# Partner rows of the 64-wide rotations: SBUF to SBUF transfers from ScalarE's queue in place of VectorE's shuffle

## The reference, cut to what matters

```python
def apply_rope(x, cos, sin):
    half = x.shape[-1] // 2
    x1, x2 = x32[..., :half], x32[..., half:]
    return jnp.concatenate([x1 * c - x2 * s, x2 * c + x1 * s], axis=-1)

qa = apply_rope(qa.reshape(b, s, A_HEADS, 64), cos_a, sin_a)   # ka, qb, kb alike
iq = apply_rope(iq.reshape(b, s, IDX_HEADS, 32), cos_i, sin_i) # ik alike
dots  = einsum('bqhd,bsd->bqhs', iq, ik) * 32 ** -0.5
score = einsum('bqhs,bqh->bqs', relu(dots), iw * 8 ** -0.5)
_, idx = lax.top_k(score, 128)            # then attention over the chosen keys
```

## Time and profile before

| | |
|---|---|
| median of 3 runs | 3537.01 us (3535.3 to 3541.0) |
| the profiled execution: its time | 3540.26 us |
| the profiled execution: its span | 3538.5 us |
| granted TensorE clock, mean | 0.985 of full speed |
| busy, share of the span: PE / DVE / ACT / POOL | 96% / 52% / 33% / 5% |
| DMA, mean | 93 GB/s |

### The profile page before, as it was taken

How to read it: one execution, slowest core, us unless ns; L and a number is a source line. 1 busy time by engine, 2 the same in 40 slices (tenths; PEclk the granted TensorE clock), 3 DMA queues, 4 the chain that set the end, 5 groups by cost and what they waited for, 6 DMA issues and landing times.

```text
span 3538.5 us, 47550 instructions
## 1 busy us (share of the span) xinstructions
PE 3399.9 (96%) x19436; PEld 2755.4 (78%) x19436; DVE 1830.4 (52%) x2634; ACT 1160.2 (33%) x1744; POOL 162.8 (5%) x136
## 2 busy tenths in 40 slices
PE   8999999999999999998899999999999999999999
PEld 7887786788888888777588888656888877578887
DVE  6667546622343234988642336895323359952233
ACT  2122434522242223342332224345222333542222
POOL 0000000000000000000000002230000023100000
PEclk8999999999999999999999999999999999999999
DMA  6555230122222222210022222210222221112222
GB/s 247 189 190 202 84 110 36 68 99 95 95 102 95 95 95 95 93 61 4 30 90 95 95 95 96 72 60 36 88 102 97 105 83 68 43 54 95 95 96 83
DMA packets 47846, 330.29 MB, mean 93 GB/s; under 512 B 5312, under 2 KB 5568, under 8 KB 9280
## 3 DMA queue, kind: packets, MB, share of 16 engines
q1 hardware_dynamic: 41216, 290.09, 22.5%
q0 software_dynamic: 6464, 37.80, 2.9%
HBM read 325.77 MB, written 2.10 MB: 93 GB/s over the span
## 4 chain that ended last, share of the span: by engine, by line
PE 84%; DVE 11%; ACT 3%; issue 1%; DMA 0%; SPq 0%; DVEq 0%; ACTq 0%
PE PS L2156 25%; PE PS L2158 25%; PE PS L2157 25%; DVE WL L2664 2%; PE PS L338 2%; DVE A L1168 1%; DVE M L1167 1%; PE PS L2234 1%; PE PS L413 1%; PE PS L395 1%; PE PS L343 1%; PE PS L1513 1%; PE PS L951 1%; PE PS L2402 1%; ACT WH L2454 0%
## 5 line engine op out<-in xcount | busy, mean ns | idle before, releaser
L2664 DVE TENSOR_TENSOR WL<-RAW,WH 128x2048 fp32r<-128x2048 f32 x255 | 593.5, 2328 | 302.9 <-ACT WH L2454 302.7
L2454 ACT ACTIVATE WH<-RAW 128x2048 fp32r<-128x2048 f32 x255 | 486.8, 1909 | 189.8 <-PE PS L2158 176.9
L2156 PE MATMUL PS<-EH,WH 128*128 128x512 f32 (+1 forms) x1408 | 535.9, 381 | 5.2 <-DVE X L2787 3.1
L2157 PE MATMUL PS<-EL,WH 128*128 128x512 f32 (+1 forms) x1408 | 534.8, 380 | 0.0
L2158 PE MATMUL PS<-EH,WL 128*128 128x512 f32 (+1 forms) x1408 | 534.8, 380 | 0.0
L2156 PE MATMUL PS<-HH,WH 128*128 128x512 f32 (+1 forms) x1312 | 503.0, 383 | 10.3 <-DVE A L2773 3.4
L2158 PE MATMUL PS<-HH,WL 128*128 128x512 f32 (+1 forms) x1312 | 496.8, 379 | 0.0
L2157 PE MATMUL PS<-HL,WH 128*128 128x512 f32 (+1 forms) x1312 | 496.4, 378 | 0.0
L2703 DVE TENSOR_TENSOR A<-SG,PS 128x512 f32 (+1 forms) x132 | 90.8, 688 | 760.6 <-ACT SG L2586 760.6
L2586 ACT ACTIVATE SG<-PS 128x512 f32<-128x512 f32 x132 | 79.3, 600 | 1062.1 <-PE PS L2158 1062.1
L2156 PE MATMUL PS<-WH,AH 128*128 128x512 f32 x1056 | 412.6, 391 | 0.3 <-DVE CV L2890 0.3
(11 more groups left out here) (436 smaller groups left out, 4222.0 us busy)
## 6 DMA issues: line engine op xcount, KB each, us to landing
RAW<-in_w SPq DMA_DIRECT2D x264, 1024.0 KB, 4.8
E<-in_ada POOLq DMA_DIRECT2D x28, 1024.0 KB, 5.1
E<-in_ada SPq DMA_DIRECT2D x4, 1024.0 KB, 11.4
G<-in_ada SPq DMA_DIRECT2D x4, 1024.0 KB, 20.8
X<-in_x SPq DMA_DIRECT2D x1, 2048.0 KB, 13.3
X<-in_xn POOLq DMA_DIRECT2D x1, 2048.0 KB, 12.1
out_x<-A SPq DMA_DIRECT2D x4, 512.0 KB, 2.7
R<-in_row_ffn_post POOLq DMA_DIRECT2D x4, 256.0 KB, 4.6
```

Of the source, the lines that this page charges most:

```text
L2156: nc.tensor.matmul(out, wh, xh, start=start, stop=False)
L2157: nc.tensor.matmul(out, wh, xl, start=False, stop=False)
L2454: nc.scalar.activation(PLACE[w][0], RAW[:, w % 2, :], ACT.Copy).then_inc(w_hi, 1)
L2664: nc.vector.tensor_tensor(PLACE[w][1], RAW[:, w % 2, :], PLACE[w][0].bitcast(F32), ALU.subtract).then_inc(w_lo, 1)
```

## The change

For the 64-wide rotations VectorE's shuffle is gone. ScalarE, having copied the two tiles of a unit, fetches the partner rows of each by four transfers of 32 partitions by 512 float32 (64 KB each), from `TURN3` to `SIN3`, on its own DMA queue. Partition p receives row p XOR 32, which a shuffle within 32 rows could not give, so the host permutation `halves_met` goes away and the tables are laid out for halves 32 rows apart. VectorE and GpSimd wait for the transfers (`moved`, two semaphores, one for each `SIN3` buffer) where they waited for the shuffle. Before it issues the transfers of rotation n, ScalarE waits until rotation n - 2 is finished. The 32-wide rotations keep the shuffle. The rest of the diff keeps counts.

```diff
@@ act_token_blocks of the first mixer, scalar block
+            t.add("proj", 21)
             t.add("w", 11)
@@ setup
+        moved = sem("moved0"), sem("moved1")
...
+        def swap_done(eng, layer, n):
+
+            if ROPED[n][2] == 64:
+                alike = [x for x, r in enumerate(ROPED) if r[2] == 64 and x % 2 == n % 2]
+                eng.wait_ge(moved[n % 2], 64 * (layer * len(alike) + alike.index(n) + 1))
+            else:
+                alike = [x for x, r in enumerate(ROPED) if r[2] == 32]
+                eng.wait_ge(swapped, layer * len(alike) + alike.index(n) + 1)
@@ pool_mix3
-            n = pool_t.add("m3")
-            pool.wait_ge(m3_loads, 64 * n)
+            layer = pool_t.add("m3") - 1
+            pool.wait_ge(m3_loads, 64 * (layer + 1))
...
-                pool.wait_ge(swapped, n_all)
+                swap_done(pool, layer, n)
                 pool.tensor_tensor(x, x, ROPE[size][0], ALU.mult).then_inc(cos_done, 1)
@@ act_mix3, behind the two copies of unit u
                     ins.then_inc(proj_evac, 1)
+                for n, r in turns_of(u):
+                    if r[2] == 64:
+                        act.wait_ge(proj_evac, proj0 + PROJ3[u][r[1]] + 1)
+                        act.wait_ge(roped, turns0 + n - 1)
+                        for p in range(0, P, 32):
+                            act.dma_start(SIN3[n % 2][p:p + 32], TURN3[n % 3][p ^ 32:(p ^ 32) + 32]).then_inc(moved[n % 2], 16)
@@ dve_mix3, rope
-                nc.vector.stream_shuffle(SIN3[n % 2], TURN3[n % 3], SWAP).then_inc(swapped, 1)
-                dve.wait_ge(swapped, turns0 + n + 1)
+                if r[2] == 32:
+                    nc.vector.stream_shuffle(SIN3[n % 2], TURN3[n % 3], SWAP).then_inc(swapped, 1)
+                swap_done(dve, layer, n)
                 nc.vector.tensor_tensor(SIN3[n % 2], SIN3[n % 2], ROPE[r[2]][1], ALU.mult).then_inc(sin_done, 1)
@@ more_arrays
-            angle = (np.arange(S, dtype=np.float32)[:, None] * inv[None]).T[row % n // 32 * 16 + row % 16]
-            sign = np.where(row % 32 < 16, -1.0, 1.0).astype(np.float32)[:, None]
+            angle = (np.arange(S, dtype=np.float32)[:, None] * inv[None]).T[row % (n // 2)]
+            sign = np.where(row % n < n // 2, -1.0, 1.0).astype(np.float32)[:, None]
@@ matrices
-                part = halves_met(part) if name in ("qa", "ka", "qb", "kb") else part
```

More of the change, by code:

```diff
@@ L1036, in act_mix3 @@
         def act_mix3(act, t, sub, h):
-            w, split, turns0, dots0 = t("w"), h["split"], t("turns"), t("dots")
+            w, split, turns0, dots0, proj0 = t("w"), h["split"], t("turns"), t("dots"), t("proj")
             def read_dots(u, c):
@@ L1082, in act_mix3 @@
             t.add("dots", len(DOTS))
+            t.add("proj", N_PROJ3)
             g0 = t("pairs")
@@ L1741, in act_mix2 @@
             t.add("w", U2)
+            t.add("proj", CHUNKS2)
             def take(to, src, *key):
@@ L3025, in out_units @@
     return down_units(w.reshape(KD, P, D)[order].reshape(D, D))
-def halves_met(w):
-    k, n = w.shape
-    return w.reshape(k, n // 64, 2, 2, 16).transpose(0, 1, 3, 2, 4).reshape(k, n)
 def padded(w, n):
```

## The result

| | median | runs from to | ratio to before, 95% interval | span profiled | clock |
|---|---|---|---|---|---|
| before, same chip | 3536.52 us | 3535.3 to 3542.92 | | 3538.5 | 0.985 |
| after | 3558.47 us | 3557.19 to 3564.79 | 1.0059 [1.0049, 1.0069] | 3563.1 | 0.98 |

The account below looks back on a forecast made before the run. The chain was 84% TensorE, held 3.1 us per layer by VectorE, which has no idle time in passes 9 to 12. Recovering that in two layers, 6.2 us, took 3537.0 to 3530.8 us; range 3526 to 3546 us.

Parts of the forecast that it names:

- In units 2 to 5 this is covered: Units 2 to 5: eight issues, 2.7 us, fit ScalarE's gap before the index dots, leaving 0.5 us.
- The signs: What would show the prediction wrong: ScalarE issues clearly over 0.4 us, landings over 5 us, or longer TensorE waits in attention.
- Everywhere earlier in the layer it waits for others: Before passes 9 to 12 VectorE waits for other engines, so shuffles saved there buy nothing.
- The clock: TensorE falls to 1.2 GHz after idle stretches; nothing in the sum, about 1 us per layer either way.
- my second rival: ScalarE's queue and landings bound passes 10 to 12, and issues overrun before index dots: 6.8 us per layer, 3550.6 us, chance 0.18.
- the loop of passes 10 to 12: Adding, issue, landing, sine, adding: at the upper bounds VectorE, and TensorE too, 4.4 us later per layer.
- The removal: Sixteen shuffles per layer go; the eight in passes 9 to 12 save VectorE 6.2 us, shorter sine products 1.2 us.
- the 0.3 us: Passes 9 to 12: saving per pair of sine products once GpSimd's cosine product is over earlier, 1.2 us per layer.
- The late waits: Passes 9 to 12: VectorE waits for second-rotation transfers, 2.3 us in pass 11, about 1 us in pass 12.
- my 3.2 us: Four transfers in a row land 3.2 us after the first issue: 3 x 0.33 us of issues plus 2.2 us landing.
- my first rival: Fetched rows come late in passes 10 to 12 and VectorE trades shuffle for wait: about 3536 us, chance 0.17.
- The size of the prize: Before the attention TensorE loses 3.1 us per layer to VectorE, 1.5 for weights and 1.6 for ScalarE's block, all recovered.

Follow-up runs that it names:

- e3: The change with transfers only for rotations of units 2 to 5, issued by GpSimd instead of ScalarE, shuffles elsewhere; 3558.42 us, 1.0055 against the kernel before.
- e2: The change with transfers only for the rotations of passes 9 to 12, shuffles in units 2 to 5; 3542.1 us, 1.0015 against the kernel before.
- e8: The change with transfers only for rotations of passes 9 to 12 and a third buffer for fetched rows; 3532.1 us, 0.9981 against the kernel before.
- e4: The change with transfers only in units 2 to 5, on ScalarE's queue, VectorE weighing three dots before the sine products; 3557.59 us, 1.0053 against the kernel before.

## Why the prediction was wrong

- **The step that failed** is "In units 2 to 5 this is covered". It had ScalarE's gap right (3.1 us) and filled it with 8 x 0.33 = 2.7 us. An issue takes 0.61, eight of them 5.0 us, and the reads of (4,0) and (5,0) came 1.5 us late by them, each with a stall of TensorE behind it. The signs named the case ("clearly over 0.4 us"), and I took the price from SP's queue, the nearer kind, where GpSimd's 0.55 was the nearer number. With 0.5 us of margin on a path that TensorE waits for, a term known only between 0 and 0.55 should have been a coin toss, not a sentence.
- **A step that was missing**: the landing in the early units. I counted the queue behind ScalarE's issues but not that behind VectorE's wait: in passes 3 to 5 the weighing of the dots follows the sine product, and ScalarE's next read follows the weighing. It made 1.7 of the 3.2 us by which (4,0) is late in the kernel after. e3, with the issues on GpSimd's queue, shows that this hold alone can bring the median of the whole loss (9.3 and 7.8 us in the layer columns). "Everywhere earlier in the layer it waits for others" was true and led me astray: an engine with idle time can still be on the path through its order.
- **The clock.** I kept it out of the sum for lack of a price. It was about half of the bill: 5.9 of 10.4 us in the first layer, 4.1 of 9.5 in the second. That is why my second rival, which had the right place (the index dots, twice per layer), gave 2.4 us for it and not 10.8: it priced the overrun, 2 x 1.2 us where 2 x 1.5 came, and neither the late copies nor what TensorE does after a stall. Its other part, the loop of passes 10 to 12, had 4.4 us per layer; over passes 9 to 12 VectorE lost nothing (42.0 us against 42.2).
- **The removal** was right: shuffles gone, 6.2 us of VectorE in passes 9 to 12, and the sine pair of pass 9 at 0.69 and 0.68 us where it was 0.69 and 1.01. In passes 11 and 12 the 0.3 us is gone too; in pass 10 it stays (0.98), where GpSimd's addition has begun at 2320.19 and the product ends 0.6 us behind it. That the 0.3 us is a whole wait that goes or stays agrees with the exclusive lock of the Trainium skill (SBUF — State Buffer, "SBUF: two separate sides"). Splits didn't get dearer by it: they take 3.37 and 3.38 us, as before.
- **The late waits** were mis-sized: 1.0, 2.7 and 3.0 us where I had 0, 2.3 and 1.0. A set of four lands later than my 3.2 us behind its first issue. In pass 11 it goes out as soon as GpSimd has finished rotation n - 2, as foreseen, and VectorE has it at 2331.71 (above), 5.1 us later; four issues are 2.45 of them. By luck the error showed little there: rotation n - 2 was finished 1.2 us after VectorE's split and not 2.7, which gave back 1.5 of the 1.9 us. So the late half went the way of my first rival, shuffle traded for wait (its 3536 us; e2 has 3542.1). ScalarE's timeline:

```profile
2326.57 2.45 ACTq L1089 DMA_DIRECT2D V<-G  x4
```

- **The size of the prize**, 3.1 us per layer, was about right: e8 has row maxima 3.6 and 3.3 us earlier, and 7 us in all.
- The rule of the Trainium skill on issuing from other engines (DMA: Bandwidth & Descriptors, "Issuing engines are not separate DMA queues") says that this saves only the sequencer's time to initiate a transfer, "usually small relative to the DMA itself". e3 agrees with the first part: with the issues on the other queue the read of (4,0) is on time again, and the landings of that stretch stay as they were (2.0 and 5.4 us, in the kernel after 2.0 and 5.3). The second part misleads here: 0.61 us of issue stands against a landing of 2.0 us.

## What to carry to other kernels

Count the small transfers before their bytes: each held its issuing queue for 0.47 to 0.61 us here, with whatever stands behind it, and no less for 32 rows than for 128. When a fix for one hold changes nothing, look in the trace for the next hold before you acquit the first; only taking both away settled it here. And ask of each covered edit how many tenths of a microsecond of cover it has on the path of TensorE: the stalls there cost about as much again in slow clock as in waiting.

## What the runs showed of the hardware

- Issue of one SBUF to SBUF transfer: 0.61 us on ScalarE's queue when four follow one another, 0.47 to 0.55 us alone; 0.50 us on GpSimd in e3; SP's load 0.33 us.
- Landing: 2.0 us for 64 KB, 2.3 us for 256 KB; 4.3 to 5.3 us beside a megabyte.
- After an idle 3.7 us TensorE's granted clock was 0.50, the lower of its two levels (1.2 GHz): matmuls of 0.63 us for some 6 us, then 0.39 again; after an idle 2.05 us the same. But in e4 a wait of 2.03 us left it at 1.00, and in e3 the slow stretch behind 3.65 us lasted 8 us.
